# A causal mask for prompt attention: product on TensorE, or addition on VectorE

## The reference

```python
s = jnp.einsum('bqhd,bkhd->bhqk', qblk, k, preferred_element_type=jnp.float32) * scale
s = s + jnp.transpose(cqblk, (0, 2, 1))[..., None] - ck_t
mask = k_pos[None, :] <= pblk[:, None]
s = jnp.where(mask, s, -jnp.inf)
p = jax.nn.softmax(s, axis=-1)
return jnp.einsum('bhqk,bkhd->bqhd', p.astype(v.dtype), v)
```

## Time and profile before

| | us |
|---|---|
| median of 3 runs (3229.58 to 3231.57) | 3229.92 |
| the profiled execution's own time | 3229.8 |
| its span, first to last instruction | 3228.3 |
| TensorE busy | 3026.4 (94%) |
| VectorE busy | 1383.6 (43%) |
| ScalarE busy | 884.3 (27%) |
| GpSimd busy | 1121.9 (35%) |

### The profile page before, as it was taken

How to read it: one execution, slowest core, us unless ns; L and a number is a source line. 1 busy time by engine, 2 the same in 40 slices (tenths; PEclk the granted TensorE clock), 3 DMA queues, 4 the chain that set the end, 5 groups by cost and what they waited for, 6 DMA issues and landing times.

```text
span 3228.3 us, 48968 instructions
## 1 busy us (share of the span) xinstructions
PE 3026.4 (94%) x19142; PEld 2833.4 (88%) x19142; DVE 1383.6 (43%) x2021; ACT 884.3 (27%) x1475; POOL 1121.9 (35%) x571
## 2 busy tenths in 40 slices
PE   5999989899999999998998988888899999999996
PEld 4978859799999999997998866657899999999995
DVE  6345381543434444446103165642444435344345
ACT  3143170241312112122212145541241312121121
POOL 1312205433333333332332255524333333333331
PEclk9999989999999999999999999999999999999998
DMA  5634612111111111111543564664111111111111
GB/s 213 251 132 154 232 63 78 52 46 46 41 43 45 45 39 45 45 39 40 167 146 145 153 140 99 178 264 177 39 46 46 40 45 45 45 40 45 45 39 68
DMA packets 99464, 295.58 MB, mean 92 GB/s; under 512 B 14000, under 2 KB 15408, under 8 KB 99104
## 3 DMA queue, kind: packets, MB, share of 16 engines
q1 hardware_dynamic: 85616, 244.52, 22.9%
q10 hardware_dynamic: 13744, 49.61, 4.5%
HBM read 253.98 MB, written 40.10 MB: 91 GB/s over the span
## 4 chain that ended last, share of the span: by engine, by line
PE 66%; issue 10%; DVE 4%; POOL 3%; ACT 2%; DMA 1%; ACTq 0%; SPq 0%; POOLq 0%; DVEq 0%
PE PS L630 57%; PE PS L919 2%; POOL WH L566 2%; PE PS L902 2%; POOL WL L569 1%; PE PS L886 1%; PE PS L887 1%; ACT PX L1320 1%; DMA KB<-in_cache_k 1%; DMA X<-in_xT 0%; PE PS L648 0%; ACT PT L1310 0%; PE PS L933 0%; DVE X L1913 0%; PE PS L965 0%
## 5 line engine op out<-in xcount | busy, mean ns | idle before, releaser
L566 POOL TENSOR_TENSOR WH<-WRAW,ZERO 128x1024 fp32r<-128x1024 f32 x214 | 410.3, 1917 | 1818.6 <-ACTq L1052 1237.1
L630 PE MATMUL PS<-HH,WH 128*128 128x342 f32 (+1 forms) x3144 | 699.3, 331 | 8.3 <-POOL WL L569 4.7
L630 PE MATMUL PS<-HL,WH 128*128 128x342 f32 (+1 forms) x3144 | 698.5, 330 | 0.0
L630 PE MATMUL PS<-HH,WL 128*128 128x342 f32 (+1 forms) x3144 | 696.3, 330 | 0.0
L630 PEld LDWEIGHTS PS<-HH,WH 128*128 128x128 f32 x3144 | 556.8, 190 | 16.9 <-issue 15.8
L630 PEld LDWEIGHTS PS<-HL,WH 128*128 128x128 f32 x3144 | 560.4, 189 | 0.2
L630 PEld LDWEIGHTS PS<-HH,WL 128*128 128x128 f32 x3144 | 559.0, 189 | 1.6
L569 POOL TENSOR_TENSOR WL<-WRAW,WH 128x1024 fp32r<-128x1024 f32 x214 | 545.6, 2550 | 16.8
L1686 DVE SCALAR_TENSOR_TENSOR FC<-FU,FCW,FC 128x1026 f32<-128x1026 f32 x96 | 239.1, 2491 | 571.5 <-ACT FC L1178 571.5
L630 PE MATMUL PS<-AH,WH 128*128 128x342 f32 (+1 forms) x1152 | 257.3, 332 | 6.3 <-DVE AL L1704 5.0
L630 PE MATMUL PS<-AH,WL 128*128 128x342 f32 (+1 forms) x1152 | 255.9, 330 | 0.0
(11 more groups left out here) (275 smaller groups left out, 3552.7 us busy)
## 6 DMA issues: line engine op xcount, KB each, us to landing
WRAW<-in_wstream SPq DMA_DIRECT2D x214, 512.0 KB, 3.5
MS<-in_mod_w SPq DMA_DIRECT2D x96, 512.0 KB, 6.8
KB<-in_cache_k SPq DMA_DIRECT2D x32, 512.0 KB, 8.8
VB<-in_cache_v SPq DMA_DIRECT2D x32, 512.0 KB, 8.2
K<-k_split SPq DMA_DIRECT2D x48, 256.0 KB
Q<-q_split SPq DMA_DIRECT2D x48, 256.0 KB
out_kv<-STG ACTq DMA_DIRECT2D x16, 545.0 KB, 3.2
MU<-in_mod_w SPq DMA_DIRECT2D x16, 512.0 KB, 12.2
```

The lines of the kernel that those rows point to most:

```text
L566: pool.tensor_tensor(WH[:, u, :], WRAW[:, u, :], ZERO[:].broadcast_to([P, UNIT]), ALU.add).then_inc(hi.sem, 1)
L630: mm = pe.matmul(PS[:, o:o + hi - lo], lhs(n), rhs[:, k, lo:hi], start=first and n == 0 and m == 0, stop=last and n == len(kts) - 1 and m ...
```

## The change

The mask products of TensorE (line 888) are left out. `s_ready` is raised by the last product of `Q2` with `K2` instead. VectorE adds `MSKB` to the diagonal block in place in PSUM before it takes the maxima, and waits for this addition by a new semaphore, `masked`.

```diff
@@ scores (TensorE)
             for lo in range(0, L, 512):
                 hi = min(L, lo + 512)
                 pe.matmul(PS[:, o + lo:o + hi], Q1[n][:, q], K1[n][:, lo:hi], start=True, stop=False)
-                pe.matmul(PS[:, o + lo:o + hi], Q2[n][0:LOGS, q], K2[n][0:LOGS, lo:hi], start=False, stop=True)
-            pe.matmul(PS[:, o + L - P:o + L], IDB[:], MSKB[:], start=False, stop=True, skip_group_check=True)\
-              .then_inc(S["s_ready"], 1)
+                mm = pe.matmul(PS[:, o + lo:o + hi], Q2[n][0:LOGS, q], K2[n][0:LOGS, lo:hi], start=False, stop=True)
+            mm.then_inc(S["s_ready"], 1)
@@ maxima (VectorE)
             dve.wait_ge(S["s_ready"], t + 1)
+            block = PS[:, 1024 * e + qt * P:1024 * e + (qt + 1) * P]
+            TT(block, block, MSKB[:], ALU.add).then_inc(S["masked"], 1)
+            dve.wait_ge(S["masked"], t + 1)
             dve.tensor_reduce(NEGM[:, t % 16:t % 16 + 1], PS[:, 1024 * e:1024 * e + (qt + 1) * P], AX_X, ALU.max,
                               negate=True).then_inc(S["max_done"], 1)
```

More of the change, by code:

```diff
@@ L353, in trunk @@
         kv_out0 kv_out1 k_hi split_out0 split_out1 v_staged v_turned v_kept v_out0 v_out1 lf_e lf_ready lf_out cum_out q_ready
-        const_rows kq_in0 kq_in1 kq_in2 kq_in3 x_kept x_again v_in0 v_in1 s_ready max_done exp_done inv_done p_normed turned0 turned1 pt_act pt_dve weighed
+        const_rows kq_in0 kq_in1 kq_in2 kq_in3 x_kept x_again v_in0 v_in1 s_ready masked max_done exp_done inv_done p_normed turned0 turned1 pt_act pt_dve weighed
         o_taken o_split0 os_ready cq_psum cq_done
```

## The result

The changed kernel took 3245.87 us (median of 5 runs, 3243.11 to 3247.27), the kernel before on the same chip 3229.58 (3225.10 to 3231.57): a ratio of 1.0051, with a 95% interval from 1.0038 to 1.0065. It is slower by 16 us where 5.6 had been forecast, and outside the range. The profiled execution took 3245.47 us (span 3244.0).

The account below looks back on a forecast made before the run. No engine was full, TensorE nearest, waiting in a ring of scores, maxima and exponential. Terms 3.0 + 0.4 + 0.5 + 0.65 + 1.1, rounded to 5.6 us, on 3229.8 gave 3235.4 us; range 3229 to 3241.

Parts of the forecast that it names:

- The addition's price: VectorE's 128-column addition with its wait was to take 0.325 us for each tile, within bounds of 0.26 and 0.455.
- dearer addition: Rival: PSUM result or chain makes VectorE's addition and wait take over 0.345 us; 3236.4 to 3241.5 us, chance 0.30.
- free wait: Rival: the reduction overlaps the addition's end on VectorE, so an addition costs 0.20 us; 3229.5 us, chance 0.03.
- The even group: Attention's even groups: additions delay step 4's transposes and last two tiles; +0.37 us each, +3.0 us for eight.
- The odd group: Attention's odd groups: the addition delays the second 896-column tile's exponential; +0.075 us each, +0.4 us for five plain ones.
- the first two tiles: The odd group's two 1024-column tiles: additions cost nothing, hidden by ScalarE's copy and over 2 us before the buffer's next use.
- Groups 1 and 13: Two odd groups with more work on VectorE: additions reach TensorE's waits more often; +0.5 and +0.65 us.
- the start: Group 0 and step 0's tiles after `rows_of_ones`: additions carry through to ScalarE and TensorE; together +1.1 us.
- the sum itself: All terms over the attention added: 5.65, rounded down to 5.6 us, giving 3235.4 us, +0.17%.
- TensorE's clock: Rival: new waits lower the clock in even groups' second half, or it rises sooner at the start; 3231 to 3239, chance 0.08.
- the ring: Attention's chain of scores, maxima, exponential, scores; the change adds one link, the period growing from 34.17 to about 34.6 us.
- wrong in kind if the granted clock in the period falls below 1.00: Sign named beforehand: a granted clock under 1.00 in the attention's period would show the forecast wrong in kind.

Follow-up runs that it names:

- e7: The change, with idle products that nobody reads ahead of four of TensorE's waits in each period; 3231.45 us, ratio 1.0007 to the kernel before.
- e2: The change without VectorE's addition and its wait, so the diagonal blocks get no mask at all; 3225.69 us, ratio 0.9988 to the kernel before.
- e5: The change, with the diagonal part of tiles wider than 512 made first and signalled apart, so VectorE adds earlier; 3235.40 us, ratio 1.0021.
- the control: The kernel before, with idle products ahead of the same four TensorE waits in each period as in e7; 3229.44 us, ratio 1.0009.
- e1: The change with TensorE's mask product and its signal kept, so the mask is added twice; 3248.30 us, ratio 1.0056 to the kernel before.
- e8: The edits of e5 and e7 together: early addition for wide tiles and four waits filled with idle products; 3228.26 us, ratio 0.9999.

## Why the prediction was wrong

- **The addition's price: right.** 0.325 us was taken from the 64-column addition and the chained pair. The rows show 0.279 to 0.300 us and 0.31 to 0.34 from its start to the reduction's, most often 0.33. The rivals of a dearer addition and of a free wait both fall.
- **The even group: the mechanism right, the size a third less.** The forecast wait of the transposes for VectorE's copy is there (0.32 us at 1977.32, where a lateness of 0.31 and a wait near 0.5 were forecast), the wait ahead of the last two tiles grew from 0.93 to 1.05, and the second one got a wait of 0.30 of its own. At full clock an even group, from its first transposes to those of the next group, takes 16.65 us (1969.27 to 1985.92) after 16.40 (1998.90 to 2015.30): +0.25 where +0.37 was summed.
- **The odd group: right in the wait, not in the end.** The wait of 1.17 us was to become 1.4 and became 1.53; the group takes 17.72 us after 17.77, so -0.05 where +0.075 was summed. From the group's first transposes the tile behind that wait starts after 11.29 us (1951.55 to 1962.84) in place of 11.21 (1981.13 to 1992.34): most of the wait's growth is that TensorE comes sooner. So also for the first two tiles, which "cost nothing": the tile of 896 columns behind them starts after 4.26 us in place of 4.30, but TensorE's wait for it grew from 1.35 to 1.51.
- **Groups 1 and 13 and the start** are not to be seen by themselves in the changed kernel: groups 1 and 13 lie under falls, and the start came out even where +1.1 was summed. Its granted clock was 0.69 after 0.66 (1839.17 to 1878.11, before 1840.91 to 1879.87), which may have paid for the additions; that isn't shown. In e7, where the clock holds, the first reductions around group 1 lie 18.44 us apart in place of 17.72: +0.7 where +0.5 was summed.
- **The step that failed is the sum itself, which was made at a granted clock of 1.00, and with it the rival "TensorE's clock".** That rival had the cause, but only part of the place, and a chance of 0.08 and a price of "some 4 us" on either side. Of the eight falls three stand in the even groups' second half, behind 1.05 and 0.32 us; five stand in the odd groups, four behind the wait of 1.51 and one behind that of 1.53. The falls cost some 1.6 us each in the groups, with one more behind, 14 of the 16 us. The argument against it was that gaps of 0.93 to 1.17 us did not lower the clock before. That shows only that they did not there; it says nothing of how far the kernel was from falling. It left out the longest wait of the period, 1.35 us at 1951.23, and the fall of the kernel before itself, with 0.72 from 2098 to 2104, right behind the 1.04 us of the earlier trace rows. The changed waits of 1.5 us and the missing products in a period were both weighed as time in the ring, and neither as a threat to the clock. And "some 4 us" pays for two or three such falls, though such a wait stands in every group.
- The condition "wrong in kind if the granted clock in the period falls below 1.00" was the right thing to look at, and it is what happened. The ring was forecast as longer by 0.445 us a period and is longer by 0.15 to 0.2: without the falls the time would have come out near e7's 3231.45, inside the range, in its lower half.

The Trainium skill, "TensorE: Matmul & The Clock Gate", section "A second HAM failure mode: psum-queue depth-cycling", tells of a kernel in which TensorE is idle for moments between groups of matmuls, and often enough that the clock goes to and fro between its two levels. The runs agree: behind waits of 1.05 to 1.53 us, a few in each period, the clock went to 0.50 and back to 1.00 here. The prediction drew on the section before it alone.

What stays open: what makes the clock fall behind one wait and not behind the same wait a period later. e2 fell with the waits of the kernel before and less work; the kernel before did not in its periods, nor did e5 with as little work and more waiting. No run here separates length, nearness, share and moment of the waits, and the falls of each kernel are those of one execution.

## What to carry to other kernels

Where TensorE runs at full clock with regular waits, a change that lengthens these, or takes work from between them, should first be priced by the clock: where waits grew by a few tenths of a microsecond, each fall behind one cost some 1.6 us. Moving a small product off TensorE isn't a gain when the replacement stands in the same ring; here the two cost 0.75 to 1.06 us a period each. If the clock does fall, idle products in the waits, into a free PSUM bank, are a cheap test and a remedy: in the control they cost 0.17% at most.

## What the hardware showed that was not expected

- The clock fell behind waits as short as 0.92 us with another of 0.22 close by (e1, at 2054 us), not each time, and came back a few us later while TensorE worked on. While it is low, TensorE's work fills its own waits: the odd group's third wait, 0.70 us, was 0.31 at 2001.83.
- VectorE's addition in place in PSUM, with a second operand from SBUF, takes 0.28 to 0.30 us for 128 columns, about as long as a reduction that reads as many (0.29).
- The 40 idle bf16 products ahead of the start (2.41 us) and the ones behind them gave the two windows of the start a granted clock of 0.92 and 1.00 in place of 0.57 and 0.60 in e8, and that was worth only 2.8 us (36.77 after 39.58). VectorE is busy 8.16 and 8.29 us of 10 there; that it sets this stretch is argued, since no run took work from it.
